# First query and key projections of a hybrid decoder layer: twelve 128-column pieces made as six blocks of seven products of sums

## The chip, the core and the metric

The kernel runs on one core of one Trainium2 chip. The metric is the device time of that core in microseconds (us), the median of several executions. The engines are named as in the profile: PE is TensorE's matrix multiply and PEld its load of the stationary operand, DVE is VectorE, ACT is ScalarE, POOL is GpSimd, and SP is SyncE, which here only issues transfers.

## What is computed

The layer runs on x of 512 positions by 1024 channels:

```
proj = x @ w_in + b_in          # queries, keys, values of three branches, forget gates, merge gates
x <- LN(alpha*x + mixer)        # three gated attention branches, merged, one output projection
x <- LN(alpha*x + cross attention to mem)
x <- LN(alpha*x + SwiGLU(x))
```

The part that matters here is the first 1536 columns of `proj`: the queries of branch A (768 columns, multiplied by 64 to the power -1/2 after the bias) and its keys (768 columns). They are wanted transposed, channels on the partitions and positions along the row, as twelve tiles of 128 channels by 512 positions (`qk` tiles 0 to 11). In the tiles of the two dilated groups the positions are also regrouped by their residue modulo 4.

## The kernel before, in words

**Numbers in two parts.** Every fp32 operand of a large product is split in two: ACT rounds it (`split`, line 1288, a CAST to fp32r), DVE takes the remainder (`rest_of`, line 1868, written as `w_lo`), and PE makes three products, high by high, low by high and high by low (`mm3`, lines 2803 to 2805). So each product has a chain behind it: transfer by SP (`load`, line 998), rounding by ACT, remainder by DVE, then PE.

**Pieces.** The columns of `w_in` go through the kernel as numbered pieces. SP loads a chunk `c` of two pieces into `raw[c % 2]`, once the remainder of the last piece of chunk `c - 2` is taken. ACT and DVE turn a piece into `w_hi[p % 2]` and `w_lo[p % 2]`. Pieces 0 to 3 and 4, 5 (`PV0`, `PV0 + 1`) give values of branch A, 6 to 17 (`PQA` to `PVBC - 1`) are the twelve pieces in question, 18 to 21 values of the other branches, and so on.

**A query or key piece** is a `tile_piece` (line 2807): 8 steps over the 1024 channels of x, each three matmuls of a stationary 128x128 weight tile against all 512 positions, 24 matmuls in all, into one PSUM bank. DVE adds the bias on the way out (`drain_piece`, lines 1921 and 1926).

**The same engines do all this in written order.** Every engine has one list of instructions, with waits on semaphores. In the stretch in question the DVE list is: remainder of piece p + 1, output of piece p, next p; after piece 3 stand the small tables (`small_tables`, lines 2049 to 2055), and after piece 9 the four remainders of the memory input `memt` (line 2068), whose roundings ACT makes at line 1381. SP's list is chunks 2 to 15 in order. Behind chunk 7 (`TAB_A_AFTER`) it waits for `mem_lo` at 4, because the bias tables are written over `memt_raw`, and then issues the 24 small transfers that build them (`tables`, line 1018). Behind chunk 9 come eight more. Then the attention of branch A starts, with pieces 18 to 30 between its scores.

**Products of sums elsewhere in the kernel.** The merge gates further on are already made in blocks of 256 columns by another scheme (`gate_product`, line 3121). x and the 1024x256 block of weights are cut into 2x2 quarters, and seven products of quarters and of sums of quarters (P1 to P7) take the place of eight. A product is 4 steps of three matmuls with 256 positions, 12 matmuls (lines 3154 to 3156). Per block POOL makes one sum of weights (line 1230), DVE two more and a third (lines 2221, 2222, 2228) and seven remainders of 128x512 (line 2213), ACT seven roundings (line 1458) and three small copies of PSUM (lines 1467, 1472, 1477), DVE two small sums (2233, 2239). The operands pass through four slots of 512 columns in `w_hi` and `w_lo`, so the rounding of product m waits until product m - 4 is done. For each block SP issues two loads of 512 KB (lines 1064 and 1065), released by the remainder of P3 two blocks earlier; that P3 is made inside the following block. The sums of x are made once (lines 2202, 2308 to 2311, 2318) and split too (lines 1441 and 2207).

## Time and profile before

| what | us |
|---|---|
| median of 3 runs (858.38 to 858.99) | 858.82 |
| the profiled execution, its own time | 858.69 |
| its span, first to last instruction | 857.0 |
| PE busy | 847.5 (99%) |
| DVE busy | 612.4 (71%) |
| ACT busy | 410.1 (48%) |
| POOL busy | 99.8 (12%) |

The span is 1.7 us shorter than the time of the same execution. A busy engine counts the overlap of pipelined matmuls as busy, so PE's 99% says that it hardly ever sat idle, not that every column was useful. What an instruction costs on PE is the distance from one start to the next, which is less than its own duration. On DVE and ACT, too, one instruction starts about 0.1 us before the former ends where nothing is waited for.

### The profile page before, as it was taken

What the parts mean: (1) busy time and instruction counts of PE and PEld (TensorE: products, weight loads), DVE (VectorE), ACT (ScalarE), POOL (GpSimd) and SP (SyncE); (2) the same over time, 40 slices, a digit from 0 to 9 for tenths busy, and PEclk for the clock granted to TensorE, in tenths of its full rate; (3) what the DMA queues carried; (4) which work ended last, traced back from release to release, by engine and by line L of the source; (5) the groups of instructions that cost most, each with busy time, mean ns of one, the idle gap of its engine ahead of it and who ended that gap; (6) DMA issues with size and microseconds to landing.
All of it is one profiled execution on the core that took longest, in us unless ns stands there. A gap on an engine that the chain in (4) does not pass through costs nothing.

```text
span 857.0 us, 14104 instructions
## 1 busy us (share of the span) xinstructions
PE 847.5 (99%) x5418; PEld 751.4 (88%) x5418; DVE 612.4 (71%) x1116; ACT 410.1 (48%) x847; POOL 99.8 (12%) x112
## 2 busy tenths in 40 slices
PE   9999999999999999999999999999999999999996
PEld 9988898877678999999889789899999999888885
DVE  5444357778565968786767689688888888877944
ACT  5121166239644555554424644366555665424521
POOL 5100000262200101010000010111111111000000
PEclk9999999999999999999999999999999999999999
DMA  9525532330002432415613111233223333651101
GB/s 303 159 98 148 124 99 75 98 99 2 1 23 86 139 127 72 148 51 234 203 56 134 65 50 50 99 99 100 99 99 100 104 120 121 248 196 50 49 25 73
DMA packets 73119, 90.47 MB, mean 106 GB/s; under 512 B 3458, under 2 KB 63638, under 8 KB 73054
## 3 DMA queue, kind: packets, MB, share of 16 engines
q1 hardware_dynamic: 72670, 89.15, 31.4%
q8 instruction: 43, 0.70, 0.3%
q0 software_dynamic: 384, 0.43, 0.3%
q14 instruction: 22, 0.18, 0.1%
HBM read 87.05 MB, written 2.52 MB: 105 GB/s over the span
## 4 chain that ended last, share of the span: by engine, by line
PE 48%; DVE 2%; issue 1%; DMA 1%; ACT 0%; DVEq 0%; POOLq 0%; POOL 0%; ACTq 0%
PE ps L2803 7%; PE ps L2805 7%; PE ps L2804 7%; PE ps L3412 7%; PE ps L3414 7%; PE ps L3413 7%; PE ps L3470 1%; PE ps L3472 1%; PE ps L3471 1%; PE ps L2840 1%; PE ps L2929 1%; DMA raw<-in_w_ffn_in 1%; PE ps L3006 0%; PE ps L2966 0%; PE ps L3355 0%
## 5 line engine op out<-in xcount | busy, mean ns | idle before, releaser
L1288 ACT CAST w_hi<-raw 128x1024 fp32r<-128x1024 f32 (+1 forms) x54 | 55.7, 1035 | 124.6 <-PE ps L2805 107.2
L2803 PE MATMUL ps<-xt_hi,w_hi 128*128 128x512 f32 (+1 forms) x256 | 99.4, 388 | 0.0
L2805 PE MATMUL ps<-xt_lo,w_hi 128*128 128x512 f32 (+1 forms) x256 | 98.8, 386 | 0.0
L1868 DVE TENSOR_TENSOR w_lo<-raw,w_hi 128x1024 fp32r<-128x1024 f32 (+1 forms) x54 | 65.2, 1208 | 47.0 <-ACT w_hi L1288 47.0
L2804 PE MATMUL ps<-xt_hi,w_lo 128*128 128x512 f32 (+1 forms) x256 | 98.8, 386 | 0.0
L3412 PE MATMUL ps<-xt_hi,w_hi 128*128 128x256 f32 x288 | 81.6, 283 | 0.1
L3413 PE MATMUL ps<-xt_hi,w_lo 128*128 128x256 f32 x288 | 81.5, 283 | 0.0
L3414 PE MATMUL ps<-xt_lo,w_hi 128*128 128x256 f32 x288 | 81.5, 283 | 0.0
L3412 PE MATMUL ps<-s_hi,w_hi 128*128 128x256 f32 x216 | 61.2, 283 | 0.0
L3413 PE MATMUL ps<-s_hi,w_lo 128*128 128x256 f32 x216 | 61.1, 283 | 0.0
L3414 PE MATMUL ps<-s_lo,w_hi 128*128 128x256 f32 x216 | 61.1, 283 | 0.0
L2547 DVE TENSOR_TENSOR w_lo<-raw,w_hi 128x512 fp32r<-128x512 f32 x72 | 49.2, 695 | 15.8 <-ACT w_hi L1689 15.4
L2803 PEld LDWEIGHTS ps<-xt_hi,w_hi 128*128 128x128 f32 x256 | 48.1, 188 | 10.1 <-issue 0.6
L2805 PEld LDWEIGHTS ps<-xt_lo,w_hi 128*128 128x128 f32 x256 | 48.1, 188 | 9.6
L2804 PEld LDWEIGHTS ps<-xt_hi,w_lo 128*128 128x128 f32 x256 | 48.1, 188 | 9.5
L3412 PEld LDWEIGHTS ps<-xt_hi,w_hi 128*128 128x128 f32 x288 | 55.3, 192 | 0.4 <-DVE w_lo L2547 0.3
L3413 PEld LDWEIGHTS ps<-xt_hi,w_lo 128*128 128x128 f32 x288 | 55.3, 192 | 0.1
L3414 PEld LDWEIGHTS ps<-xt_lo,w_hi 128*128 128x128 f32 x288 | 55.3, 192 | 0.0
L1251 POOL TENSOR_TENSOR w_t<-raw 128x512 f32<-128x512 f32 x18 | 29.5, 1637 | 174.1 <-DMA raw<-in_w_ffn_in 147.3
L1689 ACT CAST w_hi<-raw 128x512 fp32r<-128x512 f32 x72 | 44.3, 622 | 7.8 <-PE ps L3414 4.3
L1689 ACT CAST w_hi<-w_t 128x512 fp32r<-128x512 f32 x54 | 32.6, 618 | 21.7 <-DVE w_t L2555 16.5
L3412 PEld LDWEIGHTS ps<-s_hi,w_hi 128*128 128x128 f32 x216 | 41.5, 192 | 0.2 <-issue 0.2
(432 smaller groups left out, 2412.0 us busy)
## 6 DMA issues: line engine op xcount, KB each, us to landing
raw<-in_w_ffn_in SPq DMA_DIRECT2D x36, 512.0 KB, 4.4
raw<-in_w_in SPq DMA_DIRECT2D x15, 1024.0 KB, 4.8
raw<-in_w_in SPq DMA_DIRECT2D x19, 512.0 KB, 4.2
raw<-in_w_ffn_out SPq DMA_DIRECT2D x7, 1024.0 KB, 4.8
raw<-in_w_mix_out SPq DMA_DIRECT2D x4, 1024.0 KB, 4.8
raw<-in_w_ffn_in SPq DMA_DIRECT2D x4, 1024.0 KB, 5.0
out_w<-in_w_ffn_out SPq DMA_DIRECT2D x4, 1024.0 KB, 8.9
resid<-in_x SPq DMA_DIRECT2D x2, 1024.0 KB, 8.5
```

What stands on the lines that cost most here:

```text
L1251: pool.tensor_tensor(w_t1[:, :, :], w_quarter(n, 0, 1), w_quarter(n, 0, 0), ALU.subtract).then_inc(t1_done, 1)
L1288: act.copy(hi, src).then_inc(hi_done, 1)
L1689: act.copy(op_slot(m, 0), right_operand(kind, n)).then_inc(op_hi, 1)
L1868: dve.tensor_tensor(lo, src, f32(hi), ALU.subtract).then_inc(lo_done, 1)
L2547: dve.tensor_tensor(op_slot(m, 1), right_operand(kind, n), f32(op_slot(m, 0)), ALU.subtract).then_inc(op_lo, 1)
L2803: pe.matmul(dst, a_hi, b_hi, start=start, stop=False, skip_group_check=reopened)
L2804: pe.matmul(dst, a_lo, b_hi, start=False, stop=False, skip_group_check=reopened)
L2805: return pe.matmul(dst, a_hi, b_lo, start=False, stop=stop, skip_group_check=reopened)
L2840: ins = pe.transpose(ps[:, bank + hf, k * P:(k + 1) * P], src[:, t, (4 * hf + k) * P:(4 * hf + k + 1) * P], ident[:, :])
L3412: pe.matmul(dst, w_h[:, k, :], x_h[:, k, :], start=clear and k == 0, stop=False, skip_group_check=True)
L3413: pe.matmul(dst, w_l[:, k, :], x_h[:, k, :], start=False, stop=False, skip_group_check=True)
L3414: ins = pe.matmul(dst, w_h[:, k, :], x_l[:, k, :], start=False, stop=k == 3, skip_group_check=True)
```

## The change

The twelve pieces 6 to 17 become six blocks n = -6 to -1 of 256 columns (block n makes the tiles 2(n+6) and 2(n+6)+1), each by seven products as in the gate section. `gate_product`, `gate_round`, `gate_weight_sums` and their fellows are generalised to negative n. What is new ahead of the blocks are the four sums of x, their rounding and their remainders. The diff, cut to its core:

```diff
 def gate_products_in_order():
+    for n in range(-N_HEAD_BLOCK, 0):        # N_HEAD_BLOCK = (PVBC - PQA) // 2 = 6
+        inner = n > -N_HEAD_BLOCK
+        order.append(("P1", n))
+        if inner:
+            order.append(("P4", n - 1))
+        order.append(("P5", n))
+        if inner:
+            order.append(("P3", n - 1))
+        order += [("P6", n), ("P2", n), ("P7", n)]
+    order += [("P4", -1), ("P3", -1)]
@@ sync: loads of the six blocks; the rest of the list stays as it was
+            def head_weights(c):
+                n = c - PVBC // 2
+                if n < 2 - N_HEAD_BLOCK:
+                    sp.wait_ge(lo_done, last_piece(c - 2) + 1)
+                else:
+                    sp.wait_ge(g_lo, GATE_OP["P3", n - 2] + 1)
...
+                sp.dma_start(k8[:, 0:4, :], w_in[:, 0:4, n0:n0 + 256]).then_inc(gate_half[c % 2], 16)
+                sp.dma_start(k8[:, 4:8, :], w_in[:, 4:8, n0:n0 + 256]).then_inc(gate_in[c % 2], 16)
             for c in range(2, CG):
-                load(c)
+                if PQA // 2 <= c < PVBC // 2:
+                    head_weights(c)
+                else:
+                    load(c)
                 if c == TAB_A_AFTER:
                     sp.wait_ge(seg_out, 16 * 4)
                     sp.wait_ge(mem_lo, 4)
@@ gpsimd
+            pool.wait_ge(rel_ready, 3)
+            gate_weight_sums(-N_HEAD_BLOCK)
             pool.wait_ge(seg_ready, 2)
...
+            for n in range(1 - N_HEAD_BLOCK, 0):
+                gate_weight_sums(n)
@@ scalar
+            def head_blocks():
+                for kind in ("P1", "P5", "P6"):
+                    gate_round(kind, -N_HEAD_BLOCK)
+                for n in range(-N_HEAD_BLOCK, 0):
+                    first, last = n == -N_HEAD_BLOCK, n == -1
+                    if not first:
+                        gate_round("P3", n - 1)
+                        gate_seed(n)
+                        gate_round("P6", n)
+                        head_right(n - 1)
+                    gate_round("P2", n)
...
+                    gate_round("P7", n)
+                    gate_u2(n)
+                    if not last:
+                        gate_round("P1", n + 1)
+                    gate_round("P4", n)
+                    head_left(n)
+                    if not last:
+                        gate_round("P5", n + 1)
+                    gate_u3(n)
+                    if n < 4 - N_HEAD_BLOCK:
...
+                        act.copy(memt_hi[:, ks, :], memt_raw[:, ks, :]).then_inc(mem_hi, 1)
+                gate_round("P3", -1)
+                head_right(-1)
-            for p in range(3, 18):
-                split(p + 1)
...
+            for j in (1, 2, 3, 4):
+                act.wait_ge(gx_sum, 4)
+                act.copy(head_sum(j, 0), HEAD_SUMS[j - 1]).then_inc(gx_hi, 1)
+            split(PV0)
+            split(PV0 + 1)
+            head_blocks()
+            split(PVBC)
@@ vector
+            def head_blocks():
+                gate_op_rest("P1", -N_HEAD_BLOCK)
+                gate_op_rest("P5", -N_HEAD_BLOCK)
+                gate_t23(-N_HEAD_BLOCK)
+                gate_op_rest("P6", -N_HEAD_BLOCK)
+                for n in range(-N_HEAD_BLOCK, 0):
+                    first, last = n == -N_HEAD_BLOCK, n == -1
+                    if not first:
+                        gate_c22(n - 1)
+                        gate_op_rest("P3", n - 1)
+                        gate_t23(n)
+                        gate_op_rest("P6", n)
+                    gate_op_rest("P2", n)
+                    gate_op_rest("P7", n)
+                    gate_t4(n)
+                    if not first:
+                        gate_c12(n - 1)
+                    if not last:
+                        gate_op_rest("P1", n + 1)
+                    gate_op_rest("P4", n)
+                    if not last:
+                        gate_op_rest("P5", n + 1)
+                    if not first:
+                        head_second(n - 1)
+                    if n < 4 - N_HEAD_BLOCK:
+                        dve.wait_ge(mem_hi, block_no(n) + 1)
...
+                gate_c22(-1)
+                gate_op_rest("P3", -1)
+                gate_c12(-1)
+                head_second(-1)
+            dve.wait_ge(turn_lo, KT)
+            dve.tensor_tensor(A_22, A_21, A_22, ALU.add).then_inc(gx_sum, 1)
+            dve.wait_ge(gx_sum, 1)
+            dve.tensor_tensor(A_21, A_11, A_21, ALU.subtract).then_inc(gx_sum, 1)
+            dve.wait_ge(gx_sum, 2)
+            dve.tensor_tensor(A_11, A_22, A_11, ALU.subtract).then_inc(gx_sum, 1)
+            dve.wait_ge(gx_sum, 3)
+            dve.tensor_tensor(A_12, A_12, A_11, ALU.subtract).then_inc(gx_sum, 1)
...
+            rest_of(PV0)
+            for j in (1, 2):
+                dve.wait_ge(gx_hi, j)
+                dve.tensor_tensor(head_sum(j, 1), HEAD_SUMS[j - 1], f32(head_sum(j, 0)), ALU.subtract).then_inc(gx_lo, 1)
+            drain_piece(PV12 + 3)
+            small_tables()
+            rest_of(PV0 + 1)
+            for j in (3, 4):
...
+            drain_piece(PV0 + 1)
+            head_blocks()
+            rest_of(PVBC)
@@ tensor
-            for p in range(PQA, PVBC):
...
-                tile_piece(p, (6, 7, 0, 1)[n % 4])
+            for n in range(-N_HEAD_BLOCK, 0):
+                gate_product("P1", n)
+                if n > -N_HEAD_BLOCK:
+                    gate_product("P4", n - 1)
+                gate_product("P5", n)
+                if n > -N_HEAD_BLOCK:
+                    gate_product("P3", n - 1)
+                gate_product("P6", n)
+                gate_product("P2", n)
+                gate_product("P7", n)
+            gate_product("P4", -1)
+            gate_product("P3", -1)
```

`head_left` and `head_right` (ACT) write the left and the right half of a block's first tile with bias and scale. `head_second` (DVE) writes the whole second tile, after `gate_c22` and `gate_c12` have finished its two halves. The pieces 4 and 5 change places in `w_hi` and `w_lo`, so that piece 5's slot is the one that is not wanted first. P7(n) waits for `g_u2`, P4(n) for `g_u3`, P3(n) for `g_c22`, and piece 18 for its own remainder (`lo_done`), which stands behind `head_second(-1)` in DVE's list.

## Rows read from the trace of the kernel before

**Rows 1.** The page's busy line; then one of the three rows of PE's own waits.
```profile
PE 847.5 (99%) x5418; PEld 751.4 (88%) x5418; DVE 612.4 (71%) x1116; ACT 410.1 (48%) x847; POOL 99.8 (12%) x112
...
PE ps L2966 <- DVE pt L2005: 0.2, 1, 0.2
```
**Rows 2.** Timeline of PE: start us, us, instruction, around pieces 4, 6 and 18.
```profile
27.90 0.44 PE L3515 MATMUL ps<-w_hi,xt_hi 128*128 128x256 f32 x1
...
39.58 0.40 PE L2803 MATMUL ps<-xt_hi,w_hi 128*128 128x512 f32 x1
...
104.88 0.34 PE L2803 MATMUL ps<-w_hi,xt_hi 128*128 128x388 f32 x1
```
**Rows 3.** Timeline of ACT in the gate section: the copy after P6, one block apart.
```profile
298.35 0.37 ACT L1472 COPY held_odd<-ps 128x256 f32<-128x256 f32 x1 [1.12 <-PE ps L3156]
...
308.43 0.37 ACT L1472 COPY held_even<-ps 128x256 f32<-128x256 f32 x1 [2.20 <-PE ps L3156]
```
**Rows 4.** Timeline of DVE, 18 to 33 us: the list before the query pieces.
```profile
18.02 1.26 DVE L1868 TENSOR_TENSOR w_lo<-raw,w_hi 128x1024 fp32r<-128x1024 f32 x1 [0.18 <-ACT w_hi L1288]
...
27.94 2.48 DVE L1911 TENSOR_TENSOR va<-ps,bv 128x512 f32<-128x512 f32 x4 [3.35 <-PE ps L2805]
30.34 0.60 DVE L2052 TENSOR_TENSOR seg_row<-ps,seg_mask 20x448 f32<-20x448 f32 x1
...
31.58 1.23 DVE L1868 TENSOR_TENSOR w_lo<-raw,w_hi 128x1024 fp32r<-128x1024 f32 x1
```
**Rows 5.** Timelines of DVE and ACT near the gates: sums, roundings, a dependent pair.
```profile
254.21 1.22 DVE L2308 TENSOR_TENSOR xs_a<-xs_a 128x1024 f32<-128x1024 f32 x1
255.35 1.22 DVE L2309 TENSOR_TENSOR xs_a<-xs_a 128x1024 f32<-128x1024 f32 x1
...
290.85 1.41 DVE L2193 TENSOR_TENSOR mt<-mt 128x512 f32<-128x512 f32 x2
...
256.98 1.99 ACT L1441 CAST gs_hi<-xs_a 128x1024 fp32r<-128x1024 f32 x2
```
**Rows 6.** Timelines of DVE and ACT in the gate section: the small work of a block.
```profile
296.75 1.29 DVE L2213 TENSOR_TENSOR w_lo<-raw,w_hi 128x512 fp32r<-128x512 f32 x2 [0.18 <-ACT w_hi L1458]
...
298.56 0.42 DVE L2239 TENSOR_TENSOR held_even<-ps,held_even 128x256 f32<-128x256 f32 x1
...
296.11 1.13 ACT L1458 CAST w_hi<-raw 128x512 fp32r<-128x512 f32 x2
```
**Rows 7.** SP's timeline, 65 to 91 us: issues of chunk 7, the tables, chunks 8 on.
```profile
65.88 0.37 SPq L998 DMA_DIRECT2D raw<-in_w_in  x1
66.36 12.28 SPq L1018 DMA_DIRECT2D tab<-rows  x24
78.69 7.97 SPq L998 DMA_DIRECT2D raw<-in_w_in  x3
```
**Rows 8.** Line 1018 alone, 72 to 80 us: ns min/median/max, first and last start.
```profile
L1018 SPq DMA_DIRECT2D tab<-rows x15: 425/426/432, 71.7 to 78.2; - x15
```
**Rows 9.** Gate loads: SP's issue and POOL's first sum on what landed, two blocks.
```profile
294.60 0.37 SPq L1064 DMA_DIRECT2D raw<-in_w_in  x1
302.94 0.37 SPq L1064 DMA_DIRECT2D raw<-in_w_in  x1
...
297.98 1.83 POOL L1230 TENSOR_TENSOR g_t<-raw 128x512 f32<-128x512 f32 x1 [13.17 <-DMA raw<-in_w_in]
308.27 1.29 POOL L1230 TENSOR_TENSOR g_t<-raw 128x512 f32<-128x512 f32 x1 [8.47 <-DMA raw<-in_w_in]
```
**Rows 10.** Stretches by time at the kernel's end; PEclk is the third number from the right.
```profile
849.90:854.80 4.90, 0.00 (x0) 0.00 (x0) 3.61 (x6) 1.44 (x3) 0.55 (x1) 1.00 0.01 3
855.00:857.00 2.00, 0.00 (x0) 0.00 (x0) 0.00 (x0) 0.00 (x0) 0.00 (x0) 0.50 0.55 210
```
**Rows 11.** Timeline of PE, its first matmuls; then line 2859's durations, ns min/median/max.
```profile
1.58 3.36 PE L2851 MATMUL ps<-ident 128*128 128x128 f32 x14 [1.58 <-POOL ident L1142]
...
L2859 PE MATMUL ps<-w_hi,xt_hi x16: 394/399/632, 4.8 to 14.2; 128*128 128x512 f32 x16
```

More of the change, by code:

```diff
@@ new lines, in gate_seed, with gate_u2 @@
+            def gate_seed(n):
+                act.wait_ge(g_prod, GATE_OP["P1", n] + 1)
+                if n >= 0 and n % 3 == 0:
+                    act.wait_ge(merged_even, n // 3 + 1)
+                elif n == 1:
+                    act.wait_ge(merged_odd, 1)
+                act.copy(gate_c(n), gate_a(n)).then_inc(g_seed, 1)
+            def gate_u2(n):
+                act.wait_ge(g_prod, GATE_OP["P6", n] + 1)
+                if 2 - N_HEAD_BLOCK <= n < 0:
+                    act.wait_ge(proj_out, PQA + 2 * (block_no(n) - 1))
+                act.copy(gate_held(n)[:, LO], gate_c(n)).then_inc(g_u2, 1)
@@ new lines, in gate_u3, with head_left, head_right, head_out @@
+            def gate_u3(n):
+                act.wait_ge(g_prod, GATE_OP["P7", n] + 1)
+                act.copy(gate_held(n)[:, HI], gate_c(n)).then_inc(g_u3, 1)
+            def head_left(n):
+                act.wait_ge(g_prod, GATE_OP["P2", n] + 1)
+                head_out(n, LO, gate_a(n))
+            def head_right(n):
+                act.wait_ge(g_prod, GATE_OP["P4", n] + 1)
+                head_out(n, HI, gate_c(n))
+            def head_out(n, cols, src):
+                p = 2 * block_no(n)
+                dst = qk[:, p, cols]
+                if p % 6 >= 2:
+                    rows = slice(cols.start // 4, cols.stop // 4)
+                    dst = qk[:, p, :].rearrange("p (s i) -> p s i", s=4)[:, :, rows]
+                    src = src.rearrange("p (i s) -> p s i", s=4)
+                if p < T_KA:
+                    act.activation(dst, src, ACT.Identity, bias=bias_q[:, p:p + 1], scale=SCALE).then_inc(sig_left, 1)
+                else:
+                    act.activation(dst, src, ACT.Identity, bias=bias_t[:, p:p + 1]).then_inc(sig_left, 1)
@@ L1436, in gate_sum_round @@
             def gate_sum_round(j, at):
[L1438 removed]
+                act.wait_ge(gx_sum, 4 + at)
                 if j == 4:
@@ new lines, in gate_t4, with gate_c22, gate_c12 @@
+            def gate_t4(n):
+                dve.wait_ge(g_lo, GATE_OP["P6", n] + 1)
+                dve.tensor_tensor(second_sum(n), gate_quarter(n, 1, 0), second_sum(n), ALU.subtract).then_inc(g_t4_done, 1)
+            def gate_c22(n):
+                dve.wait_ge(g_u3, block_no(n) + 1)
+                dve.tensor_tensor(gate_held(n)[:, HI], gate_b(n), gate_held(n)[:, HI], ALU.add).then_inc(g_c22, 1)
+            def gate_c12(n):
+                dve.wait_ge(g_prod, GATE_OP["P3", n] + 1)
+                dve.wait_ge(g_u2, block_no(n) + 1)
+                dve.tensor_tensor(gate_held(n)[:, LO], gate_b(n), gate_held(n)[:, LO], ALU.add).then_inc(g_c12, 1)
@@ new lines, in head_second @@
+            def head_second(n):
+                p = 2 * block_no(n) + 1
+                dve.wait_ge(g_c22, block_no(n) + 1)
+                dve.wait_ge(g_c12, block_no(n) + 1)
+                dve.wait_ge(sig_left, 2 * block_no(n) + 2)
+                dst, src = qk[:, p, :], gate_held(n)
+                if p % 6 >= 2:
+                    dst = dst.rearrange("p (s i) -> p s i", s=4)
+                    src = src.rearrange("p (i s) -> p s i", s=4)
+                if p < T_KA:
+                    dve.tensor_scalar(dst, src, bias_t[:, p:p + 1], SCALE, ALU.add, ALU.mult).then_inc(proj_out, 2)
+                else:
+                    dve.tensor_scalar(dst, src, bias_t[:, p:p + 1], None, ALU.add).then_inc(proj_out, 2)
```

340 lines of the change are left out of this document (172 added, 168 removed).

## The prediction

> **What bounds the kernel now.** I read the busy line first: PE is busy for 847.5 us of a span of 857.0 [rows 1]. Then the waits of PE alone. There are three of them, 2.0 us together, of which one of 0.2 stands in the rows and the longest (1.6) is at the very start [rows 1]. So there is no slack on PE anywhere: what PE is spared comes off the time, and every wait that PE gets is added to it. Third, PE's timeline around the changed stretch. Piece 4 starts at 27.90, the twelve query and key pieces run from 39.58, and piece 18 starts at 104.88 [rows 2]. Last, the lists of DVE, ACT and SP ahead of that stretch and under it, because the change puts a good deal of work there, in front of things that PE waits for.
>
> **PE's own work.** Twelve pieces take 104.88 - 39.58 = 65.30 us, 5.44 each, 0.227 per matmul of 512 positions [rows 2]. For the new products the gate section has the price: the copy after P6 comes at 298.35 and, one block of seven products later, at 308.43, so a product is 10.08 / 7 = 1.44 us and a matmul of 256 positions 0.12 [rows 3]. It waits for PE both times, and PE does not wait there. The six blocks are 42 products, 60.48 us. This term is 60.5 - 65.3 = **-4.8 us**. One eighth of 65.3 would be 8.2, and the smaller matmuls give 3.4 of it back, since half the positions cost 0.120 and not 0.113.
>
> The Trainium skill ("TensorE: Matmul & The Clock Gate", section "Back-to-back issue gap") gives an isolated gap of N / 2.4 + 2.5 ns, 109 ns at 256 and 216 at 512. An estimate by that page is a gain of 7.1 us for this term, and the sum below would end at 870.0. Its figures lie under what the rows show at both sizes, and the rows decide.
>
> **The start, on DVE and ACT.** Today piece 4's remainder is made long before PE wants it. After the change DVE first makes four sums of 128x1024. It can begin at 18.02 + 1.14 = 19.16 [rows 4]. Such a sum is 1.22 long and the next independent one starts 1.14 later; a dependent pair of 0.69 takes 1.41, 0.72 apart instead of 0.60, so a dependence costs about 0.13 [rows 5, 6]. Three steps of 1.27 and a last 1.22 end at 24.2. ACT waits for all four and then rounds them ahead of piece 4: two take 1.99, so 0.95 a step [rows 5], and piece 4's rounding runs from 28.0 to 29.1. DVE's remainder is 1.23 [rows 4], so PE starts piece 4 at 30.4 instead of 27.90: **+2.5**.
>
> Piece 4 issues for 48 x 0.12 = 5.76, to 36.2. Meanwhile DVE has, behind that remainder, two remainders of sums (2.3), four outputs of values (2.4) and the small tables (31.58 - 30.34 = 1.2), and only then piece 5's remainder, 1.23 [rows 4]: ready at 30.3 + 2.3 + 2.4 + 1.2 + 1.2 = 37.4, so **+1.3**. Piece 5 issues to 43.2. Its output is two instructions of 0.6 on DVE, and P1's remainder (0.69, two in 1.29 [rows 6]) stands behind them. With 0.16 for the last matmul to end (its length of 0.28 less 0.12) PE can start P1 of the first block at 45.3: **+2.0**. Against 39.58 the blocks start 5.8 late. Everything between is hidden: weight sums of the first block by POOL, and the other two remainders of sums under piece 5.
>
> **Inside the blocks.** DVE has per block seven remainders, three weight sums (0.6 a step each), two small sums (0.42 each), one output of 128x512 and, in the first four, a memt remainder: about 8 us of 10.08. ACT has seven roundings (two in 1.13 [rows 6]), three small copies (0.37 [rows 3]), two outputs and a memt rounding: about 6. The order is that of the gates, where PE waited for nothing, so I cost this at nothing. POOL's first sum is concurrent with DVE's in the gates too.
>
> **The last block's load, on SP.** This is the big term. SP's list is kept: chunk 7, then `mem_lo` at 4, 24 table transfers, then chunk 8. Before, `mem_lo` came early, chunk 7 went out at 65.88, the tables from 66.36 to 78.64 and chunk 8 at 78.69, with its piece 16 wanted only at 94 [rows 7]. After, chunk 8 is the last block, n = -1. The four memt remainders now go one to a block, each behind `g_u3`, that is, behind the block's P7. Block -2 starts at 45.3 + 7.2 + 3 x 10.08 = 82.8 (the first block has five products ahead of the second's first). P7 of block -3 has ended by then. With its copy (0.3), the memt rounding (0.6), the remainder (0.7) and the matmul's end, `mem_lo` reaches 4 at 84.6. The 24 issues cost 12.28 with a transfer in flight, and (78.2 - 71.7) / 14 = 0.464 each without [rows 7, 8]. With nothing in flight I take 24 x 0.464 = 11.1: chunk 8 is issued at 95.8. Half of it lands 3.4 us after its issue in one gate load and 5.3 in another [rows 9]. I take 3.9, close to the lower because little is in flight, a bit above because the last tables are ahead of it. Rounding and remainder add 1.4: P1 of the last block can start at 101.1. PE would have come to it at 45.3 + 7.2 + 4 x 10.08 = 92.8. So **+8.2**, with bounds 6.5 (issues of 0.43 [rows 8] and 3.4 to land) and 11.3 (12.28 and 5.3). Its other half and its sums are wanted four products later and are in time. Chunks 9 and 10 and the eight further tables also move behind this, but piece 18 needs chunk 9 some 14 us later.
>
> **The clock.** The granted clock is full until the end, and 5.1 us after the last matmul it is at 0.50 (PE ended at 849.9, full up to 854.8, half from 855.0 [rows 10]). An idle PE for 8.2 us in the middle should lose it as well, and pays on resuming. The price is bounded by the start: first matmul at 1.58, the first of 512 positions at 4.8 still 632 ns against a median of 399, all later ones fast [rows 11]. So at most 3.5 us at half speed, 1.75 lost; the other end is 0. I take **+1.6**, since the start is the only example of a cold PE under load. The start's new waits of 2.5, 1.3 and 2.0 have matmuls between them, and I take them not to lose it.
>
> The Trainium skill (same page, section "Why this matters for your kernels") warns against idle gaps between bursts of matmuls because the clock falls back to half. The trace agrees at the kernel's end, with the 0.50 above, and no run here shows a gap in the middle.
>
> **The end of the stretch.** P4 of the last block has no product between it and P7, whose result ACT must copy first: 0.16 + 0.37, **+0.5**. Then P3's result, and behind it on DVE `gate_c12` (0.42), `head_second` (0.7) and piece 18's remainder (about 1.0, a shorter row than 1.23), with the matmul's end **+2.3** before piece 18 starts, where it now follows at once. Bounds of both together 2.0 to 3.2.
>
> **Sum.** -4.8 + 5.8 + 8.2 + 1.6 + 0.5 + 2.3 = +13.6. The profiled execution took 858.7 (span 857.0 and 1.7 around it), which is the median of 858.82 within 0.1: **872.3 us**. The bounds of the terms (start 4.9 to 6.5, the rest as given) reach from 867.3 to 876.6.
>
> **Rivals.**
> - *Last load in time.* If the table issues do not hold it (they go out sooner, or cost far less when nothing else moves), the terms of 8.2 and 1.6 fall: 862.5. Against it stands 12.28 us for 24 issues [rows 7]. Chance 0.10. The Trainium skill ("DMA: Bandwidth & Descriptors", section "Issuing engines are not separate DMA queues") says that the time a sequencer takes to initiate a transfer is usually small relative to the transfer itself, which would give this case. The issues of line 1018 contradict it for small transfers.
> - *More waits inside the blocks.* DVE is at 8 of 10 us, and a late memt rounding stands in its list ahead of P3's remainder. A wait of 0.5 to 1 us in each of five blocks gives 875 to 877. For it: POOL's sum stretches a concurrent DVE instruction. Against: P3's slack is over 1.5 us. Chance 0.10.
> - *Faster.* DVE's dependent sums and ACT's four roundings are the hinge of the start. If that chain were ready by 27.9, that is, if ACT were free to round piece 4 first, the start would cost nothing, and if SP's list held nothing either, -4.8 + 2.8 remains: 856.7. It decides itself at one point, whether the roundings that PE waits for come ahead of the new ones, and the lists as written say no. Chance 0.03.
> - *The change does not do what it says*, for instance the sums are hidden and PE's saving is lost to slower 256-position matmuls: 858.8. Chance 0.02.
>
> **Numbers.** The main case has 0.75. Range 867.0 to 876.6: it leaves out the first, the third and the fourth rival and takes in part of the second. A measurement can tell 0.2% (1.7 us). Slower 0.95, faster 0.03, same 0.02.
>
> **What would show it.** PE's waits should name `w_lo` behind ACT before pieces 4 and 5 and the first P1 (2.5, 1.3, 2.0), one wait of some 8 us before P1 of the last block with SP's 24 issues right before its load, and 2 to 2.5 before piece 18; the clock below full right after the 8 us. Between, copies after P6 every 10.08. If the load of chunk 8 goes out before 92, the main case is wrong; if blocks are over 10.3 apart, the second rival holds.

## The result, and the profile after

| what | before | after |
|---|---|---|
| median, us | 858.90 | 877.82 |
| the profiled execution, its own time | 858.69 | 877.61 |
| its span | 857.0 | 875.8 |
| PE busy | 847.5 (99%) | 848.9 (97%) |

The change makes the kernel slower: the ratio is 1.0216, with a 95% interval of 1.0196 to 1.0236. The prediction said 872.3 with a range of 867.0 to 876.6. So the direction was right, and the time lies 1.2 us above the range. Three of the four executions took 877.11 to 878.03 us, and the fourth, with a mean granted clock of 0.748, took 1046.66 us, which counts in the median of 877.82 but not in the ratio.

The busy line of the page after, against [rows 1]:

```profile
PE 848.9 (97%) x5634; PEld 762.2 (87%) x5634; DVE 647.0 (74%) x1179; ACT 435.3 (50%) x911; POOL 110.0 (13%) x118
```

PE is busy for 1.4 us more than before, although its work is less. That is a first sign that part of it ran slowly. The waits of PE alone, kernel after (columns: what waits and on which line, what it waits for, then us in total, number of times, longest):

```profile
PE ps L3114 <- DVE w_lo L2185: 11.8, 3, 9.4
PE ps L3717 <- DVE w_lo L2015: 2.9, 2, 1.9
PE ps L2995 <- DVE w_lo L2015: 2.4, 1, 2.4
PE ps L3043 <- POOL ident L1223: 1.6, 1, 1.6
PE ps L3114 <- ACT held_a L1500: 0.6, 1, 0.6
PE ps L3205 <- DVE pt L2137: 0.2, 1, 0.2
PE ps L3557 <- ACT xt_hi L1382: 0.2, 1, 0.2
```

The three waits of 2.0 us together that PE had before are still there: the 1.6 for `ident`, at the very start, and the two of 0.2 at the foot of the list. New are 11.8 + 2.9 + 2.4 + 0.6 = 17.7 us, and the largest single one is 9.4. PE's timeline shows where each of them stands (start us, duration, instruction; in brackets the wait before it):

```profile
30.74 0.39 PE L3717 MATMUL ps<-w_hi,xt_hi 128*128 128x256 f32 x1 [1.86 <-DVE w_lo L2015]
...
37.79 0.39 PE L3717 MATMUL ps<-w_hi,xt_hi 128*128 128x256 f32 x1 [1.03 <-DVE w_lo L2015]
...
45.77 0.39 PE L3114 MATMUL ps<-xt_hi,w_hi 128*128 128x256 f32 x1 [1.98 <-DVE w_lo L2185]
...
49.28 0.39 PE L3114 MATMUL ps<-a_hi,w_hi 128*128 128x256 f32 x1 [0.37 <-DVE w_lo L2185]
...
103.61 0.58 PE L3114 MATMUL ps<-xt_hi,w_hi 128*128 128x256 f32 x1 [9.44 <-DVE w_lo L2185]
...
104.21 0.41 PE L3116 MATMUL ps<-xt_lo,w_hi 128*128 128x256 f32 x1
104.42 0.41 PE L3114 MATMUL ps<-xt_hi,w_hi 128*128 128x256 f32 x1
...
116.84 0.36 PE L3114 MATMUL ps<-xt_hi,w_hi 128*128 128x256 f32 x1 [0.55 <-ACT held_a L1500]
...
119.67 0.28 PE L3116 MATMUL ps<-a_lo,w_hi 128*128 128x256 f32 x1
...
122.31 0.41 PE L2995 MATMUL ps<-w_hi,xt_hi 128*128 128x388 f32 x1 [2.36 <-DVE w_lo L2015]
```

Against [rows 2]: piece 4 starts at 30.74 (27.90 before), the first block at 45.77 (piece 6 at 39.58), the last block at 103.61, and piece 18 at 122.31 (104.88). Note the two lines after that of 103.61: matmuls of 256 positions stand 0.21 apart there, where it is 0.12 elsewhere. The stretches of the same trace say why (columns: window, its length, busy us and count of PE, PEld, DVE, ACT, POOL, then the granted clock, DMA share, GB/s):

```profile
45.80:94.00 48.20, 47.83 (x396) 47.60 (x396) 37.72 (x62) 27.07 (x57) 5.83 (x4) 1.00 0.29 84
94.00:103.60 9.60, 0.18 (x2) 0.00 (x0) 1.25 (x2) 1.91 (x4) 1.27 (x1) 0.75 0.49 140
103.60:108.90 5.30, 5.29 (x24) 5.29 (x25) 4.39 (x8) 1.80 (x5) 0.00 (x0) 0.50 0.31 83
108.90:119.80 10.90, 10.35 (x85) 10.12 (x84) 4.74 (x8) 5.07 (x10) 0.00 (x0) 1.00 0.82 137
...
122.31:126.01 3.70, 3.70 (x12) 3.70 (x13) 0.73 (x1) 0.00 (x0) 0.00 (x0) 0.55 0.51 130
```

The blocks run at the full clock, 2.4 GHz (1.00), up to 94. Then comes the long wait, in the middle of which the clock falls to its lower level of 1.2 GHz (0.50). It stays there for the first 5.3 us of work, in which 24 matmuls fit. The last line is the second place: after a wait of only 2.4 us, piece 18 starts at half clock again, and 12 matmuls fit into 3.7 us where the kernel before had 22.

The long wait has its cause in SP's list, as a timeline shows (compare [rows 7], where the same issues came 20 us earlier):

```profile
76.64 0.37 SPq L1095 DMA_DIRECT2D raw<-in_w_in  x1
...
85.85 12.15 SPq L1084 DMA_DIRECT2D tab<-rows  x24
98.05 0.43 SPq L1095 DMA_DIRECT2D raw<-in_w_in  x1
```

and DVE's list says what SP waited for between 76.64 and 85.85, the last remainder of the memory input:

```profile
85.07 0.69 DVE L2256 TENSOR_TENSOR memt_lo<-memt_raw,memt_hi 128x512 fp32r<-128x512 f32 x1
```

ACT's rounding of what the load brought ends the chain: the load is issued at 98.05 and rounded from 101.69 on, 3.64 later.

```profile
101.69 0.62 ACT L1479 CAST w_hi<-raw 128x512 fp32r<-128x512 f32 x1 [9.98 <-DMA raw<-in_w_in]
```

**The span's 18.8 us, place by place.**

| place | from the lines above | us | predicted |
|---|---|---|---|
| PE's own work | the first five blocks' copies after P6 stand 10.08 apart | -4.8 | -4.8 |
| start, to the first P1 | 45.77 - 39.58 | +6.2 | +5.8 |
| first block | wait of 0.37 before P6, and about 0.3 spread up to 94.0 | +0.7 | 0 |
| wait before the last block | 103.61 - 94.0 | +9.6 | +8.2 |
| half clock after it | last nine products from 103.61 to 119.79, 16.2; less 9 x 1.44 and the wait of the next line | +2.6 | +1.6 |
| P4 behind P7 | 0.55 | +0.6 | +0.5 |
| wait before piece 18 | 122.31 - 119.79 | +2.5 | +2.3 |
| rest of the kernel | 875.8 - 122.31 = 753.5, against 857.0 - 104.88 = 752.1 | +1.4 | 0 |
| sum | | +18.8 | +13.6 |

### The profile page after: what moved, and what is told of

The parts are those of the page before. It is cut to its first block, busy times and chain, and to the rows that moved or that the text cites. A ratio compares the mean times of both kernels' runs of the same rounds, so it can differ in the third digit from the quotient of the medians.

```text
span 875.8 us, 14765 instructions
## 1 busy us (share of the span) xinstructions
PE 848.9 (97%) x5634; PEld 762.2 (87%) x5634; DVE 647.0 (74%) x1179; ACT 435.3 (50%) x911; POOL 110.0 (13%) x118
## 4 chain that ended last, share of the span: by engine, by line
PE 91%; DVE 4%; issue 2%; ACT 1%; SPq 1%; DMA 0%; POOL 0%; DVEq 0%; POOLq 0%; ACTq 0%
PE ps L2995 12%; PE ps L2997 12%; PE ps L2996 12%; PE ps L3614 7%; PE ps L3615 7%; PE ps L3616 7%; PE ps L3114 5%; PE ps L3116 5%; PE ps L3115 5%; PE ps L3168 3%; PE ps L3245 3%; PE ps L3205 2%; SPq L1084 1%; PE ps L3672 1%; PE ps L3674 1%
## 5 line engine op out<-in xcount | busy, mean ns | idle before, releaser
L2015 DVE TENSOR_TENSOR w_lo<-raw,w_hi 128x1024 fp32r<-128x1024 f32 (+1 forms) x42 | 50.4, 1204 | 45.5 <-ACT w_hi L1376 45.4
L3614 PE MATMUL ps<-xt_hi,w_hi 128*128 128x256 f32 x288 | 81.6, 283 | 0.0
L3615 PE MATMUL ps<-xt_hi,w_lo 128*128 128x256 f32 x288 | 81.5, 283 | 0.0
L3616 PE MATMUL ps<-xt_lo,w_hi 128*128 128x256 f32 x288 | 81.5, 283 | 0.0
L3114 PE MATMUL ps<-xt_hi,w_hi 128*128 128x256 f32 x216 | 62.6, 290 | 12.0 <-DVE w_lo L2185 11.4
L3116 PE MATMUL ps<-xt_lo,w_hi 128*128 128x256 f32 x216 | 62.2, 288 | 0.0
L3115 PE MATMUL ps<-xt_hi,w_lo 128*128 128x256 f32 x216 | 62.2, 288 | 0.0
L2995 PE MATMUL ps<-xt_hi,w_hi 128*128 128x512 f32 (+1 forms) x160 | 62.0, 388 | 0.0
L2997 PE MATMUL ps<-xt_lo,w_hi 128*128 128x512 f32 (+1 forms) x160 | 61.5, 384 | 0.0
L2996 PE MATMUL ps<-xt_hi,w_lo 128*128 128x512 f32 (+1 forms) x160 | 61.4, 384 | 0.0
L2739 DVE TENSOR_TENSOR w_lo<-raw,w_hi 128x512 fp32r<-128x512 f32 x72 | 49.0, 694 | 16.7 <-ACT w_hi L1836 16.2
L2185 DVE TENSOR_TENSOR w_lo<-raw,w_hi 128x512 fp32r<-128x512 f32 x60 | 41.7, 710 | 25.3 <-ACT w_hi L1479 24.9
L3615 PEld LDWEIGHTS ps<-xt_hi,w_lo 128*128 128x128 f32 x288 | 55.3, 192 | 0.1
L3616 PEld LDWEIGHTS ps<-xt_lo,w_hi 128*128 128x128 f32 x288 | 55.3, 192 | 0.0
L3114 PEld LDWEIGHTS ps<-xt_hi,w_hi 128*128 128x128 f32 x216 | 42.5, 197 | 12.9 <-DVE w_lo L2185 11.8
```

Source lines behind the costliest of these rows:

```text
L2015: dve.tensor_tensor(lo, src, f32(hi), ALU.subtract).then_inc(lo_done, pieces_counted(p))
L2739: dve.tensor_tensor(op_slot(m, 1), right_operand(kind, n), f32(op_slot(m, 0)), ALU.subtract).then_inc(op_lo, 1)
L2995: pe.matmul(dst, a_hi, b_hi, start=start, stop=False, skip_group_check=reopened)
L2996: pe.matmul(dst, a_lo, b_hi, start=False, stop=False, skip_group_check=reopened)
L2997: return pe.matmul(dst, a_hi, b_lo, start=False, stop=stop, skip_group_check=reopened)
L3114: pe.matmul(dst, w_h[:, k, :], x_h[:, k, :], start=clear and k == 0, stop=False, skip_group_check=True)
```

## The experiments

All kernels are edits of the kernel after, and none of them leaves work out. Two theories had to be told apart for the long wait: that the last block's load is held by the 24 issues on SP, which stand ahead of it (my theory), or that it comes late anyway, because its buffer comes free late or because the tables' bytes are in its way. For what stands beyond the wait, the question was the clock. The times below are medians of all executions of a kernel, and the ratio is to the kernel before on the same chip. The kernel before itself took 858.8 us in the set of experiments 1 to 4, 859.1 in that of 5 to 7 and 859.75 in that of 8 and 9, so between sets the ratios are to be compared, not the medians.

**1. The tables behind the last load instead of ahead of it.**

```diff
-TAB_A_AFTER, TAB_B_AFTER = 7, 9
+TAB_A_AFTER, TAB_B_AFTER = 8, 9
```

> The 24 table transfers go out behind chunk 8 (the last block's load) instead of before it; nothing else changes. Theory (SP's queue holds the last load, and the long wait costs the clock): the wait of 9.4 us before the last block's P1 goes, and with it the slow matmuls behind it (2.6 us), so 877.8 - 9.6 - 2.6 = 865.6 us. Whether the second stretch at half clock, behind the gap of 2.4 us before piece 18, stays (865.6) or goes as well (864.2) tells if that gap alone is enough to lose the clock. Rival (the load would be late without the tables too, because it is released late): the wait stays at 4 us or more, 870 us or above.

Measured: 864.29 us, ratio 1.0062 (1.0047 to 1.0077). 13.5 us come back, 71% of the loss. SP's timeline of this kernel:

```profile
87.02 0.37 SPq L1095 DMA_DIRECT2D raw<-in_w_in  x1
...
88.06 12.19 SPq L1084 DMA_DIRECT2D tab<-rows  x24
```

The load goes out at 87.02, 11 us earlier, the 24 issues take 12.19 as before, and no wait of PE before the last block is left. So the buffer was free at 87.0 and the load had only been queued behind the tables. The 13.5 are more than the wait of 9.6. Piece 18 starts at 110.6 instead of 122.31, 11.7 earlier, which is the wait and the half clock of 2.6 behind it, less a start that is 0.3 later. Behind piece 18 the kernel takes 862.2 - 110.6 = 751.6 instead of 753.5: in this kernel the wait of 2.4 before piece 18 did not lose the clock. Another wait did. One stretch of its trace:

```profile
30.80:34.40 3.60, 3.57 (x17) 3.58 (x18) 3.60 (x5) 0.00 (x0) 0.00 (x0) 0.53 0.00 0
```

Right behind the first wait, before piece 4, PE issues 17 matmuls in 3.6 us at a clock of 0.53. The kernel after had the same wait there and kept the clock. It cost only 0.3 (the first P1 at 46.07 against 45.77). PE waits for DVE again further on, and what it loses ahead of such a wait it doesn't lose again: the wait of 1.03 before piece 5 is gone in this trace, and the one of 1.98 before the first P1 is unchanged.

**2. Matmuls in the wait.** To price the clock alone, 36 matmuls on an unused bank, whose result nobody reads, stand ahead of the last block. They fill most of the wait and remove nothing.

```diff
             for n in range(-N_HEAD_BLOCK, 0):
+                if n == -1:
+                    for _ in range(36):
+                        pe.matmul(ps[:, 2, 0:P], ident[:, :], ident[:, :], start=True, stop=True)
                 gate_product("P1", n)
```

> 36 fp32 matmuls of the identity (about 0.23 us each at full clock, 8.3 us together, into an unused bank) are put on TensorE in front of the last block's P1, inside the wait of 9.6 us. The wait itself stays. Theory (half clock comes from the idle time and costs 2.6 us behind it): the clock stays full, P1 starts at the same 103.6, the block's nine products take 13.6 us instead of 16.2, 875.2 us, or 873.8 if the second low stretch of 1.4 us was a consequence of the first. Rival (the clock is low for another reason, or its price is not what I take): 877.8, or more by what the matmuls add.

Measured: 875.51 us, ratio 1.0186 (1.0169 to 1.0203). Timeline of PE:

```profile
94.00 8.20 PE L3122 MATMUL ps<-ident 128*128 128x128 f32 x72
...
103.53 0.39 PE L3114 MATMUL ps<-xt_hi,w_hi 128*128 128x256 f32 x1 [1.32 <-DVE w_lo L2185]
...
114.42 0.36 PE L3114 MATMUL ps<-xt_hi,w_hi 128*128 128x256 f32 x1 [0.55 <-ACT held_a L1500]
...
119.89 0.66 PE L2995 MATMUL ps<-w_hi,xt_hi 128*128 128x388 f32 x1 [2.36 <-DVE w_lo L2015]
```

(The page counts each of the 36 as two, in fp32.) P1 of the last block starts where it did, 103.53 against 103.61, but P4 follows 10.9 later instead of 13.2. So the half clock behind the long wait is worth 2.3 us here, and it is PE's idleness that brings it. The wait before piece 18, 2.36 as before, still has the half clock behind it:

```profile
120.00:121.00 1.00, 1.00 (x4) 1.00 (x5) 0.62 (x1) 0.00 (x0) 0.00 (x0) 0.50 0.04 12
```

So that second stretch does not come from the first: a wait of 2.4 us can be enough for it. It is not always, as experiment 1 shows, whose wait before piece 18 is just as long.

**3. The start in another order.** ACT rounds piece 4 ahead of the four sums. DVE takes piece 5's remainder ahead of the small tables, and the first block's remainders ahead of piece 5's output.

```diff
+            split(PV0)
             for j in (1, 2, 3, 4):
...
-            split(PV0)
             split(PV0 + 1)
@@ vector
             drain_piece(PV12 + 3)
-            small_tables()
             rest_of(PV0 + 1)
+            small_tables()
+            gate_op_rest("P1", -N_HEAD_BLOCK)
+            gate_op_rest("P5", -N_HEAD_BLOCK)
             for j in (3, 4):
...
+            gate_t23(-N_HEAD_BLOCK)
+            gate_op_rest("P6", -N_HEAD_BLOCK)
             drain_piece(PV0 + 1)
```

(the four calls for the first block go out of `head_blocks()`)

> Only the order at the start changes: ScalarE rounds piece 4 before the sums of x, VectorE takes piece 5's remainder before the small tables, and the first block's weight operands before piece 5's output. Theory (the start is late by 6.2 us because new work stands ahead of work that TensorE waits for): pieces 4 and 5 start as in the kernel before, P1 of the first block at about 39.6 to 40, and P6's wait of 0.4 goes: 877.8 - 6.2 - 0.7 = 870.9 us, the later wait of 9.6 unchanged, since it hangs on the blocks' own pace. Rival (the late start is absorbed by the SP queue's wait): no gain, 877 us.

Measured: 870.81 us, ratio 1.0134 (1.0119 to 1.0149), 7.0 less than the kernel after. The waits named for the start are gone, and what is left for `w_lo` of line 2185 is one wait, the long one:

```profile
PE ps L3114 <- DVE w_lo L2185: 9.7, 1, 9.7
```

P1 of the last block starts at 97.71, 5.9 earlier than before this edit, although it waits as long as ever. Everything ahead of the last load, the memory input's remainders included, moved forward with PE. The first P1 starts at 40.33, 5.4 earlier; the rest of the 5.9 is P6's wait and the spread in the first block. So what is saved at the start is not eaten up by the long wait.

**4. The end in another order.** Piece 18 is rounded ahead of `head_right(-1)` and its remainder taken right behind P3's, ahead of `gate_c12` and `head_second`.

```diff
                 gate_round("P3", -1)
+                split(PVBC)
                 head_right(-1)
@@ vector
                 gate_op_rest("P3", -1)
+                rest_of(PVBC)
                 gate_c12(-1)
```

(and both go where they stood behind `head_blocks()`)

> Only the end changes: piece 18 is rounded before the last block's right half is written, and its remainder is taken before the last two sums. Theory: the gap of 2.4 us before piece 18 goes, and the clock is not lost a second time (1.4 us): 877.8 - 3.8 = 874.0 us. If the second low stretch comes from something else, 875.4.

Measured: 873.34 us, ratio 1.0167 (1.015 to 1.0184), 4.5 less. The wait before piece 18 is gone from PE's list. 4.5 is more than the 2.5 of that wait. Part of it is the half clock behind the wait, which went too: piece 18 starts at 119.11, and from there to the end of the span of 870.7 it is 751.6, 1.9 less than in the kernel after. The rest of this trace, of an execution 0.9 under the median, differs in ways that the edit did not aim at. Its start is 0.8 earlier, and the low clock behind the long wait covers only 3.2 us of work instead of 5.3, so that P4 follows P1 after 12.3 us and not 13.2. Against that, the first P1's wait, which the kernel after had as well, now did lose the clock, and the last block's P1 comes 1.1 later behind the first P1 than there. One stretch, right behind the first P1's wait:

```profile
45.80:49.20 3.40, 3.40 (x18) 3.40 (x18) 3.32 (x5) 2.03 (x4) 1.60 (x1) 0.52 0.02 6
```

and the same stretch of the first experiment's kernel, which has the same wait of 2.0 ahead of it:

```profile
45.80:49.20 3.40, 3.13 (x24) 2.93 (x24) 3.31 (x5) 1.94 (x4) 1.61 (x1) 1.00 0.09 28
```

18 matmuls against 24, with 0.37 us of waiting in the latter.

**5. All three orders together.**

> The three changes of order together: tables behind chunk 8, the start's order, the end's order. Theory: nothing of the change is left but its saving on TensorE of 4.8 us and the wait of 0.6 before P4 of the last block, with no stretch at half clock after the first microseconds: 858.8 - 4.8 + 0.6 = 854.6 us, faster than the kernel before, with runs closer together than those of the changed kernel. Rival (the blocks themselves cost more than the gate section shows, or the waits move to the next place): 857 us or more.

Measured: 856.94 us (12 executions), ratio 0.9972 (0.9962 to 0.9981). This kernel is 0.28% faster than the one before and 20.9 us faster than the one after. Its waits, beside the three that the kernel before had, and its timeline at the three places:

```profile
PE ps L2995 <- DVE w_lo L2015: 0.7, 1, 0.7
PE ps L3114 <- ACT held_a L1500: 0.6, 1, 0.6
```

```profile
28.09 0.44 PE L3717 MATMUL ps<-w_hi,xt_hi 128*128 128x256 f32 x1
...
39.77 0.28 PE L3114 MATMUL ps<-xt_hi,w_hi 128*128 128x256 f32 x1
...
101.87 0.41 PE L2995 MATMUL ps<-w_hi,xt_hi 128*128 128x388 f32 x1 [0.69 <-DVE w_lo L2015]
```

Piece 4 and the first block start within 0.2 of the kernel before (27.90 and 39.58 in [rows 2]), piece 18 starts 3.0 earlier. So PE's term is real: 60.5 us for the blocks, 101.87 - 39.77 = 62.1 with the waits of 0.6 and 0.7 and 0.3 more that is spread. The 854.6 that I expected was missed by 2.3 (by 2.0 if it is worked out from the 859.1 that the kernel before took in this set). In the profiled execution (856.22) 0.2 of them are in the start and 0.7 in the last wait. The part behind piece 18 takes 854.5 - 101.87 = 752.6, against 752.1 before and 751.6 in experiment 1, so that without any low clock it varies by 1 us, without a cause that I have found. Why the median lies another 0.7 higher is open too. The clock is full there, with 21 matmuls where the kernel after had 12:

```profile
101.87:105.57 3.70, 3.70 (x21) 3.70 (x22) 1.75 (x3) 0.24 (x1) 0.00 (x0) 1.00 1.15 228
```

**6 and 7. The tables where they were, with another cause removed.** Experiment 1 moved both the issues and the tables' bytes away from the load. In experiment 6 the memory input is split before the blocks, so that the issues come early, ahead of the load:

```diff
+            act.wait_ge(mem_in, 16)
+            for i in range(4):
+                act.copy(memt_hi[:, 2 * i:2 * i + 2, :], memt_raw[:, 2 * i:2 * i + 2, :]).then_inc(mem_hi, 1)
             head_blocks()
```

(and on DVE the four remainders ahead of `drain_piece(PV0 + 1)`; both are taken out of the blocks)

> The changed kernel with the four roundings and remainders of the memory input taken ahead of the blocks; the 24 tables stay before chunk 8. Theory (what holds the tables is mem_lo, and what holds the last load is the tables' issue time of 12.2 us): the tables go out right behind chunk 7, at 77.5, chunk 8 at 89.7, and P1 of the last block starts 5.6 us later as in the changed kernel, at 95.3 where it could start at 94.0: a wait of about 1.3 us, clock kept there: 864.3 + 1.3 = 865.6 us, give or take 1.4 for a half-clock stretch at one of the short gaps. Rival (the tables wait for something else): the wait stays at 9 us, 877 us.

In experiment 7 only eight of the 24 transfers stay ahead of the load:

```diff
                 if c == TAB_A_AFTER:
...
                     tables(tab1, rows1, 0, N_AH, SEG1, 256)
+                if c == TAB_A_AFTER + 1:
                     tables(tab4, rows4, 0, N_AH, SEG4, P)
                     tables(tab16, rows16, 0, N_AH, SEG16, P)
```

> The changed kernel with 8 of the 24 table transfers before chunk 8 and 16 behind it. Theory (the wait is issue time on SP, transfer by transfer): 8 issues cost 4 us from 85.8, chunk 8 goes out at 89.9 instead of 98.05, P1 at 95.4, a wait of about 1.4 instead of 9.6: 864.3 + 1.4 = 865.7 us. Rival (the wait is the bytes of the tables in front of the load): these eight carry half of the bytes, so half of the wait stays, 4 to 5 us, and with it the clock's price, 869 us or more.

Measured: 865.91 us, ratio 1.0079 (1.0066 to 1.0092), and 866.50 us, ratio 1.0085 (1.0069 to 1.0101). SP's timelines, first of 6, then of 7:

```profile
76.36 0.37 SPq L1095 DMA_DIRECT2D raw<-in_w_in  x1
...
77.62 11.21 SPq L1084 DMA_DIRECT2D tab<-rows  x24
88.88 0.56 SPq L1095 DMA_DIRECT2D raw<-in_w_in  x1
```

```profile
85.55 3.63 SPq L1084 DMA_DIRECT2D tab<-rows  x8
89.23 0.43 SPq L1095 DMA_DIRECT2D raw<-in_w_in  x1
...
90.25 8.44 SPq L1084 DMA_DIRECT2D tab<-rows  x16
```

In both the load goes out at about 89, with all of the tables' bytes in front of it in one and half of them on either side in the other. In experiment 6 no wait before the last block is left, in experiment 7 one of 0.9:

```profile
94.83 0.39 PE L3115 MATMUL ps<-xt_hi,w_hi 128*128 128x256 f32 x1 [0.94 <-DVE w_lo L2186]
```

ACT begins to round what the load brought at 92.68 and 92.89, 3.80 and 3.66 us after its issue, against 3.64 in the kernel after. So the bytes in front of it cost 0.2 at most. What decides is the moment at which SP comes to the load: its place in the list, the event that SP waits for, and the count of issues ahead of it. Changing any one of the three takes away all of the wait of 9.4 or, in experiment 7, nine tenths of it. That both kernels are still 1.5 to 2.0 us slower than that of experiment 1, by the ratios, fits that 0.9 and the clock: both have a stretch of 3.4 us at 0.50 at piece 18, where experiment 1 has none.

**8. The end earlier still.** On top of 5, P3 of the last block is rounded and its remainder taken before `head_second(-2)`, and piece 18 is rounded right behind `gate_u3(-1)`.

```diff
-                    if not last:
-                        gate_round("P5", n + 1)
+                    gate_round(*(("P3", -1) if last else ("P5", n + 1)))
                     gate_u3(n)
+                    if last:
+                        split(PVBC)
@@ vector
-                    if not last:
-                        gate_op_rest("P5", n + 1)
+                    gate_op_rest(*(("P3", -1) if last else ("P5", n + 1)))
...
                 gate_c22(-1)
-                gate_op_rest("P3", -1)
+                rest_of(PVBC)
```

> As the three orders together, with P3 of the last block rounded and its remainder taken one step sooner, so that piece 18's remainder comes sooner too. Theory: the wait of 0.7 us before piece 18 (and the 0.2 around it) goes, nothing else moves: 856.9 - 0.9 = 856.0 us. Rival (what kept the three orders 2.3 us above my sum lies behind piece 18): no gain, 856.9.

Measured: 856.28 us (5 executions), ratio 0.9959 (0.9947 to 0.9972). By its median it is 0.66 under experiment 5, but the intervals overlap, and the profiled spans are 854.6 and 854.5. The wait before piece 18 is gone, and another has come, in the scores of branch A behind it:

```profile
PE ps L3165 <- DVE stat_a L2109: 1.4, 3, 0.9
```

What PE was spared at 102 it waits for at 119 to 127, for the statistics of the scores, which DVE makes. Behind piece 18, which starts at 101.04, the kernel takes 753.6, which is 752.2 and the new waits of 1.4. So this edit moved a wait and did not remove it.

**9. Tables and start, with the end as it was.**

> Tables behind chunk 8 and the start's order, with the end as in the changed kernel: one gap of 2.4 us before piece 18, behind 60 us in which TensorE never sat idle for more than 0.6. It gives the gap's price by itself. If a gap of 2.4 us costs the clock only by chance, 856.9 + 1.7 = 858.6 us with the clock kept and 860.0 with it lost, the runs lying between the two; if it costs it always, 860.0 and a low stretch in the profile.

Measured: 858.05 us (11 executions), ratio 0.9977 (0.9966 to 0.9988). Its wait before piece 18 is 2.4 again, and its profile has the low clock behind it:

```profile
104.90:108.10 3.20, 3.20 (x12) 3.20 (x11) 0.00 (x0) 0.00 (x0) 0.00 (x0) 0.50 1.10 360
```

This profile is of an execution of 858.72. The mean granted clock of each of the 11 executions splits them: at 0.995 there are three with a mean of 858.65 us, at 0.999 five with a mean of 857.71. The other three lie at 0.997 and 0.998, with times between 858.05 and 858.99. The mean also holds the end of the span, where PE has nothing to do and the clock is low in every trace, for 1.9 us (experiment 1) to 5.0 us (experiment 7). A mean of 0.999 over 856 us leaves room for at most 2.6 us at 0.50, less than one stretch of 3.4, so those five executions kept the clock. A mean of 0.995 means 7.7 to 9.4 us at 0.50, more than any such end, so those three lost it, as the traced one did (3.4 at piece 18 and 4.7 at the end). The middle ones can be either. These are estimates from the means, since only one execution was traced. So the same wait loses the clock in some executions and not in others, and the difference is about 0.9 us. The median of 858.05 lies under both expected values, 0.6 from the lower, which fits that most executions kept the clock.

## Why the prediction was wrong in size

**The step that failed is the clock, "+1.6", with "at most 3.5 us at half speed, 1.75 lost".** Measured: 4.0 us in two places. Behind the long wait 5.3 us of work ran at half clock and cost 2.3 (experiment 2) to 2.6 (the table). At piece 18 a wait of 2.4 lost the clock a second time. The table gives 1.4 to that, and it is less sure: the part behind piece 18 took 753.5 us with the low stretch, and 752.6, 752.1 and 751.6 without it (experiment 5, the kernel before, experiment 1), and experiment 9's two groups of executions are 0.9 apart. All traces together say the same: behind piece 18 it is 753.0 to 753.5 in the six that have the low stretch there (the kernel after, experiments 2, 3, 6, 7 and 9) and 751.6 to 752.6 in the four that have neither it nor a new wait (the kernel before, experiments 1, 4 and 5), 1.3 apart on average. So it is 0.9 to 1.9, and the whole term 3.2 to 4.5, where the sum had 1.6 and allowed 1.75 at most. The other terms with bounds stayed inside them. Two assumptions were wrong. I bounded the price by the start of the kernel [rows 11], as if the first work of the kernel and work behind a wait paid alike. And I took waits of 2 to 2.5 us not to lose the clock, with nothing in the trace that had such a wait in the middle. The Trainium skill ("TensorE: Matmul & The Clock Gate", section "Why this matters for your kernels") warns of idle gaps between bursts. The traces agree for the gap of 9.6 us, and experiment 2 shows that filling it gives the clock back. They also show it, in some executions, for gaps of about 2 us. With this one term at its measured 4.0 the sum would be 872.3 + 2.4 = 874.7, inside the range. The other terms were short by 1.4, 0.7, 0.4, 0.2 and 0.1, all on the same side, and together they lead to 877.5, for a profiled execution of 877.6.

**The last block's load, "+8.2", measured 9.6.** The mechanism is shown by experiments 1, 6 and 7. The tables' issues began at 85.85, not 84.6 (+1.2), since the blocks had started 0.5 late and lost 0.7 in the first of them. They and the gap behind them took 12.2, not 11.2 (+1.0): I had taken the faster rate of [rows 8] where the 12.28 of [rows 7] was right. The load landed 0.3 sooner than assumed (3.64 against 3.9). Rounding and remainder took 1.9, not 1.4 (+0.5), and PE itself came to the last block 1.2 later, at 94.0. The sum of these is +1.2, the rest is rounding. The bounds of 6.5 and 11.3 held it.

**The start, "+5.8", measured 6.2.** Its three steps were 2.5, 1.3 and 2.0. Measured are 2.84, and then 37.79 - 30.74 - 5.76 = 1.3 and 45.77 - 37.79 - 5.76 = 2.2 to the next two. The four sums end at 24.55 and not 24.2, as DVE's last sum shows, and ACT's four roundings then push piece 4:

```profile
23.33 1.22 DVE L2278 TENSOR_TENSOR xt_raw<-xt_raw 128x1024 f32<-128x1024 f32 x1
```

Experiments 3 and 5 confirm the rest. With the order mended no wait is left at the start, and the first P1 comes at 40.33 and 39.77, against 39.58 before. The 0.8 and 0.2 that remain stand ahead of piece 4, which starts at 28.66 and 28.09 without a wait, so PE came that much later out of pieces 0 to 3. In the kernel after it was 1.0 later there (30.74 less the wait of 1.86, against 27.90), which the wait hid. No run shows the cause of this.

**"Inside the blocks ... I cost this at nothing".** The blocks n = -5 to -2 follow each other at 10.08 with no named wait. The first block had one of 0.37, and this line shows why, beside the 0.69 that the same instruction takes elsewhere:

```profile
47.61 1.61 DVE L2185 TENSOR_TENSOR w_lo<-a_t,w_hi 128x512 fp32r<-128x512 f32 x1
```

```profile
47.07 1.60 POOL L1268 TENSOR_TENSOR g_t<-raw 128x512 f32<-128x512 f32 x1 [7.67 <-DVE a_t L2193]
```

POOL's sum ran at the same time, and DVE's remainder was 0.9 longer. The remainder that ended the long wait has the same neighbour and took 1.21, which is the 0.5 named above:

```profile
102.35 1.21 DVE L2185 TENSOR_TENSOR w_lo<-raw,w_hi 128x512 fp32r<-128x512 f32 x1 [11.25 <-ACT w_hi L1479]
```

```profile
101.74 1.27 POOL L1268 TENSOR_TENSOR g_t<-raw 128x512 f32<-128x512 f32 x1 [19.91 <-DMA raw<-in_w_in]
```

That the two engines hold each other up is read from these overlaps, and no run took POOL's sum away. In experiment 5 POOL's sum of the first block is just as long (39.30 to 40.91), but the same remainder starts when only 0.2 of it is left, and takes 0.79:

```profile
40.67 0.79 DVE L2185 TENSOR_TENSOR w_lo<-a_t,w_hi 128x512 fp32r<-128x512 f32 x1 [0.92 <-ACT w_hi L1479]
```

Not every DVE instruction is held: the one before the remainder, at 46.84 in the kernel after, overlaps POOL's sum by 0.45 and kept its 0.68. The second rival ("more waits inside the blocks", 0.5 to 1 us in each of five) names this mechanism, but it struck in the first block alone, and 0.4 of the 0.7 is the wait. The other 0.3 is spread over the first five blocks without a row that explains it.

**The end, "+0.5" and "+2.3"**: 0.6 and 2.5, inside their bounds. **PE's own work, "-4.8"**: 42 products at 1.44, as forecast.

**The other rivals.** "Last load in time" fell: 9.4 us of waiting. The Trainium skill ("DMA: Bandwidth & Descriptors", section "Issuing engines are not separate DMA queues") calls the time to initiate a transfer usually small relative to the transfer. These runs do not bear that out for small ones: 24 issues kept SP for 11.2 to 12.2 us, about 0.47 to 0.51 each, where such a transfer lands 1.9 to 2.2 us after its issue. "Faster" was priced at 856.7, if both lists held nothing. As a description of the kernel after it is wrong, but its price is right: experiment 9, where just those two lists are mended and the end is left, has a ratio of 0.9977, which is 2.0 us under the kernel before (1.7 by the medians), where the rival had 2.0.

## What to carry to other kernels

When a step is made cheaper on the bound engine but needs new operands, read the other engines' lists at its two ends first: here the saving of 4.8 us was real, and three places in the order of ACT, DVE and SP, none of which adds or removes work, were worth 21 us. A transfer queued behind an event and behind a row of small issues is late by the event plus about half a microsecond for each of them, so the load that the bound engine wants next goes ahead of them. And a short wait of the bound TensorE costs more than its length: price one of about 2 us at 0 to 1.7 us more for the clock (an estimate: half of the 3.4 us that a low stretch lasted), and work on all of them, since with one gone the loss can come at another, as in experiments 1 and 4.

## What the runs showed of the hardware

- A wait of 1.8 to 2.4 us with matmuls on either side loses the clock in some cases and keeps it in others. The kernel after kept it through two such waits at the start and lost it at piece 18, where it fell only at 122.6, 0.3 us after PE had gone on. The first experiment lost it behind the first wait and kept it at the other places. The fourth lost it behind the wait before the first block, and the sixth there and at piece 18. The second, third and seventh lost it at piece 18 alone, among waits of that length, and the ninth, whose only such wait that is, in some executions. The traces without such waits, those of the kernel before and of experiments 5 and 8, show no loss between the start and the end. The trace of each loss behind such a wait shows some 3.4 us at 0.50. I have no rule for which wait it strikes. What it costs depends on what follows: 0.3 us where PE waits again soon (experiment 1), 0.9 to 1.9 where it works on.
- Behind the wait of 9.6 us the low clock lasted for 5.3 us of work. With the part that lay in the wait, from 98.8 on, it was 10.2 us. The granted clock of the wait itself was full for its first half. In experiments 3 and 4 the low clock around the long wait lasted 10.2 us as well, but began at 92.3 and 96.8, so that 4.8 and 3.2 us of work fell under it. Its cost goes with that: P1 to P4 of the last block took 13.2 us in the kernel after, 13.0 in experiment 3, 12.3 in experiment 4, and 10.9 at full clock in experiment 2.
- A DVE subtraction of 128x512 took 1.61 us instead of 0.69 with a POOL sum of the same shape beside it, 1.21 beside another (POOL's took 1.27), and 0.79 where they overlapped by 0.2 only. Another DVE instruction, with 0.45 of overlap, took its usual 0.68.
